# The second norm's inverse root moved from ScalarE and VectorE to ScalarE alone, and the prompt's top-8 rounds one place earlier

## The chip, the cores and the metric

The kernel runs on one core of a Trainium2 chip. The metric is the device time of one execution in microseconds (us), as the median of several runs. TensorE multiplies matrices, VectorE (DVE in the trace) and ScalarE (ACT) work on vectors, GpSimd (POOL) issues the indirect DMAs, SyncE (SP) the others. Each engine has its own instruction stream and waits for the others by semaphores.

## What is computed

Two layers of a mixed attention, convolution and MLP backbone with an expert-choice mixture of experts, for 256 prompt tokens and 1024 latent tokens of width 1024. The change concerns the second RMS norm of each layer and what routes the tokens:

```python
def rmsnorm(x, g):
    xf = x.astype(jnp.float32)
    y = xf * lax.rsqrt(jnp.mean(xf * xf, axis=-1, keepdims=True) + EPS)
    return (y * g.astype(jnp.float32)).astype(x.dtype)

def expert_choice_ffn(h, p):
    b, n, d = h.shape
    cap = (EC_FACTOR * n) // N_EXPERTS
    logits = jnp.einsum('bnd,de->bne', h, p['w_router']).astype(jnp.float32)
    aff = jax.nn.softmax(logits, axis=-1)
    gates, idx = lax.top_k(aff.transpose(0, 2, 1), cap)
    xs = jax.vmap(lambda hb, ib: hb[ib])(h, idx)
    ...

def layer_step(x, mod, rope, ctx_ckv, ctx_krope, p):
    ...
    x = x + g1 * mix
    h = rmsnorm(x, p['norm2_g']) * (1 + sc2) + sh2
    x = x + g2 * expert_choice_ffn(h, p)
    return x, ckv, kpe
```

With 16 experts and a factor of 2 each expert takes 32 prompt rows and 128 latent rows.

## The kernel before

The tokens stand in ten tiles of 128, two of the prompt and eight latent ones. In the stage that the change touches they are taken in the order latent first: s = 0 to 7 are latent tiles, s = 8 and 9 the prompt's. For each tile TensorE projects the mixer's output with w_out (L1177, 32 matmuls of 512 columns), VectorE multiplies by the gate and adds the residual (`add_residual`, L2030 and L2032, which gives XO), TensorE turns XO (L1189), and ScalarE takes the sum of squares of XO (`mean_square`, L1600) and copies the turned tile (`copy_sums`, L1562; for prompt tiles also L1565, for latent tiles VectorE does the second half, L2001). ScalarE then takes the square root of mean square plus eps (`root`, L1603) and signals `ss2_ready`. VectorE takes the reciprocal, rstd (`normalise_sums`, L2040), and writes the normalised tile XN (L2046); of the prompt's tiles ScalarE writes it (`normalise_prompt_sums`, L1610).

Beside that runs the router. TensorE multiplies the turned, not yet normalised tile by the weights in four parts (`route`, L1203), ScalarE copies the parts (`copy_parts`, L1574, behind `root` in its stream), TensorE adds them up (`add_parts`, L1218), and VectorE makes the logits by multiplying by rstd (`row_maxima`, L2007), takes the row maximum and its negative (L2010, L2011, nmax). ScalarE takes the exponents (`exponents_of`, L1580), VectorE their reciprocal sum and the affinities (`affinity`, L2016, L2019), TensorE turns the affinities (L1226) and ScalarE copies them (L1589) into `aff`: 32 partition rows for the latent tokens (two halves of 512 for each of 16 experts) and 16 more for the prompt's.

The selection is VectorE's. One round takes the eight largest of each partition row (MAX8, L2051), finds their positions (L2056) and overwrites them with -1 (L2057). The latent rows need 16 rounds, numbered 0 to 15; the prompt's rows need four, and these are done in the same instructions, on 48 partitions instead of 32. `PROMPT_ROUND` is the first of the four. They can start only when tile 9's affinities are there. The order on VectorE is written out by hand: rounds 0 and 1, rstd of tile 8, rounds 2 and 3, tile 8's logits, first half of tile 9's residual, tile 8's affinities, round 4, second half of tile 9's residual, rounds from 5 to `PROMPT_ROUND - 2`, rstd and logits of tile 9, MAX8 of round `PROMPT_ROUND - 1`, tile 9's affinities, the rest of that round, the four rounds with the prompt, the prompt's positions (L2099), one round, the prompt's index tables out of PSUM (idx_q, L2103 to L2105), the rest of the rounds, and the lists of the latent rows (L2107 to L2119).

Behind the tables GpSimd gathers the chosen prompt rows (L718, four indirect DMAs) from xnp_dram, TensorE turns them (`turn_prompt_rows`, L1239, in its stream behind the transposes of the lists, L1327 to L1330) and ScalarE modulates them (L1594). Behind the lists GpSimd gathers expert 0's latent rows (L723), TensorE turns them (L1342), ScalarE and VectorE modulate them (L1654, L2136), and the experts start (L1357). In layer 0 TensorE also computes part of layer 1's modulation in this tail (L1295, L1304).

ScalarE computes functions out of a loaded table; `ACT_TABLE_LOAD` instructions are put in by the build ahead of an ACTIVATE whose function is not in the loaded table.

Of the kernel before, what the change touches and what calls it, by code (L numbers as in the profile page):

```python
# [75 lines left out]
OUT_ORDER = list(range(PT, NT)) + list(range(PT))  # L76
ROUTED = [4, 5, 6, 7, 8, 9]
HALF = NS // 2
PROMPT_ROUND = 8
XQ_BANK = (4, 6, 2, 4)  # L80
PROMPT_LIST = slice(CAP_P + 8 * PROMPT_ROUND, 2 * CAP_P + 8 * PROMPT_ROUND)

# [32 lines left out]
def backbone(nc, x_prompt, x_sample, cache_ckv, cache_krope, c, c_ctx, w_ada, b_ada, norm1_g, norm2_g, w_in,  # L115
# [8 lines left out]
    with ExitStack() as ctx:  # L124
# [3 lines left out]
        def sem(name):  # L128
            return ctx.enter_context(nc.semaphore(name))
# [246 lines left out]
        h2_turned = sem("h2_turned")  # L376
        h2_ready = sem("h2_ready")
        log_summed = sem("log_summed")
        row_scalar_ready = sem("row_scalar_ready")
        lexp_ready = sem("lexp_ready")  # L380
        aff_ready = sem("aff_ready")
        aff_turned = sem("aff_turned")
# [1021 lines left out]
        def _(act):  # L1404
# [10 lines left out]
            for l in range(DEPTH):  # L1415
# [160 lines left out]
                def exponents_of(t):  # L1576
                    if not 0 <= t < NT:
                        return
                    act.wait_ge(row_scalar_ready, at(l, NT + PT, t + 1 + max(0, t + 1 - NT + PT)))
                    act.activation(logit[:, t % 2, :], logit[:, t % 2, :], ACT.Exp, bias=nmax[:, t % 2:t % 2 + 1],  # L1580
                                   accum_out=psum_row[:, t % 2:t % 2 + 1]).then_inc(lexp_ready, 1)

# [14 lines left out]

                def mean_square(s):
                    act.wait_ge(xo_ready, at(l, NT, s + 1))
                    own.done(act.activation(junk_d, XO[s % 2], ACT.Square, accum_out=ss_act[:, s:s + 1]))  # L1600

                def root(s):
                    act.activation(ss[:, s:s + 1], ss_act[:, s:s + 1], ACT.Sqrt, bias=eps[:, :], scale=1.0 / D)\  # L1603
                        .then_inc(ss2_ready, 1)

                def normalise_prompt_sums(s):

                    act.wait_ge(row_scalar_ready, at(l, NT + PT, s + 1 + s - NT + PT))
                    act.wait_ge(xn_stored[s % 2], at(l, 16 * NT // 2, 16 * (s // 2)))
                    act.activation(XN[s % 2], XO[s % 2], ACT.Copy, scale=rstd[:, s:s + 1]).then_inc(xn2_ready, 1)  # L1610

                for s in range(NT + 1):
                    copy_sums(s - 1)
                    if s:
                        root(s - 1)
                    copy_parts(s - 1)
                    exponents_of(s - 1)
                    copy_affinity(s - 1)
                    if s > NT - PT:
                        normalise_prompt_sums(s - 1)  # L1620
                    if s < NT:
                        mean_square(s)
# [76 lines left out]
        def _(dve):  # L1699
# [46 lines left out]
            for l in range(DEPTH):  # L1746
# [256 lines left out]
                def row_maxima(t):  # L2003
                    tile = OUT_ORDER[t]
                    i, g = t % 2, 0 if tile < PT else 1
                    dve.wait_ge(sel_summed, at(l, NT, t + 1))
                    dve.scalar_tensor_tensor(out=logit[:, i, :], in0=PS[:, 7, 0:E], scalar=rstd[:, t:t + 1],  # L2007
                                             in1=const_row[:, g, :], op0=ALU.mult, op1=ALU.add).then_inc(logit_ready, 1)
                    dve.wait_ge(logit_ready, at(l, NT, t + 1))
                    step(dve.tensor_reduce(pmax[:, i:i + 1], logit[:, i, :], AX, ALU.max))  # L2010
                    dve.tensor_scalar(nmax[:, i:i + 1], pmax[:, i:i + 1], -1.0, None, ALU.mult).then_inc(row_scalar_ready, 1)  # L2011

                def affinity(t):
                    tile, i = OUT_ORDER[t], t % 2
# [22 lines left out]

                def normalise_sums(s):
                    dve.wait_ge(ss2_ready, at(l, NT, s + 1))
                    step(dve.reciprocal(rstd[:, s:s + 1], ss[:, s:s + 1]))  # L2040
                    if s >= NT - PT:
                        dve.sem_inc(row_scalar_ready, 1)
                        return
                    if s >= 2:
                        dve.wait_ge(xn_stored[s % 2], at(l, 16 * NT // 2, 16 * (s // 2)))
# [194 lines left out]
```

## Time and profile before

| | us |
|---|---|
| median of 3 runs | 2514.78 (2513.65 to 2514.93) |
| the profiled execution's own time | 2514.64 |
| its span in the profile | 2512.9 |
| TensorE (PE) busy | 2402.1, 96% of the span |
| VectorE (DVE) busy | 771.1 |
| ScalarE (ACT) busy | 510.4 |

The chain of work that ended last is 93% TensorE and 3% VectorE. A row of the groups by line names line, engine, operation, what is written and read, the shapes and the count, then the busy time, the mean of one in ns, and the idle time of the engine before them. A row of the timeline is start, duration, engine and line; in brackets the idle time before it and what ended it. A row of the stretches gives for each engine the busy time and the count of instructions.

### The profile page before, as it was taken

The page shows a single profiled execution, that of the slowest core. Times are in us where ns is not written, and L with a number is a line of the kernel's source. Part 1 is how long each engine was busy: PE and PEld are TensorE (multiplying, and loading weights), DVE is VectorE, ACT ScalarE, POOL GpSimd, SP SyncE. Part 2 cuts the span into 40 slices and gives each one's busy share as a digit, 9 for nine tenths or more (in the row PEclk, how much of TensorE's full clock was granted, in tenths as well). Part 3 has the DMA queues.
Part 4 walks back from the last instruction along what each step waited for, and adds up shares of the span by engine and source line. Part 5 has one row for each costly group of instructions (what it writes and reads, how often), then busy time and mean ns, then how long its engine had stood idle before and what let it go on. Part 6 is the DMA issues. An engine that isn't in the chain of part 4 may idle for free.

```text
span 2512.9 us, 31572 instructions
## 1 busy us (share of the span) xinstructions
PE 2402.1 (96%) x13056; PEld 1587.0 (63%) x13056; DVE 771.1 (31%) x1553; ACT 510.4 (20%) x1038; POOL 277.1 (11%) x434
## 2 busy tenths in 40 slices
PE   6999999999998999999989999999999959999996
PEld 4545556666444788788845455666654448888785
DVE  2401334455237211111142022445543361111113
ACT  3310122222234201101142102212223331011103
POOL 3000011201000111211110000110000001211211
PEclk8999999999999999999999999999999979999998
DMA  9100224301426788888850002330012258888888
GB/s 327 34 17 5 84 74 133 88 10 51 176 101 234 264 276 273 273 277 271 271 171 17 21 0 84 110 110 11 9 65 106 87 193 271 277 274 271 277 282 302
DMA packets 165724, 388.07 MB, mean 154 GB/s; under 512 B 14544, under 2 KB 24984, under 8 KB 165632
## 3 DMA queue, kind: packets, MB, share of 16 engines
q1 hardware_dynamic: 142864, 332.48, 38.8%
q0 software_dynamic: 22768, 54.29, 9.0%
q8 instruction: 66, 1.08, 0.2%
q14 instruction: 26, 0.21, 0.1%
HBM read 339.09 MB, written 47.65 MB: 154 GB/s over the span
## 4 chain that ended last, share of the span: by engine, by line
PE 93%; DVE 3%; DMA 2%; ACT 1%; issue 1%; SPq 0%; DVEq 0%; POOLq 0%; ACTq 0%
PE PS L1357 11%; PE PS L1364 11%; PE PS L1177 11%; PE PS L1389 9%; PE PS L930 8%; PE PS L1023 7%; PE PS L1088 7%; PE PS L884 5%; PE PS L873 5%; PE PS L1070 4%; PE PS L1035 4%; PE PS L1383 2%; PE PS L984 1%; PE PS L1342 1%; PE PS L1048 1%; DMA r<-in_x_prompt_dram 1%
## 5 line engine op out<-in xcount | busy, mean ns | idle before, releaser
L1357 PEld LDWEIGHTS PS<-r,ring 128*128 128x128 f32 x2048 | 281.5, 190 | 16.8 <-issue 16.8
L1177 PE MATMUL PS<-ring,mix 128*128 128x512 f32 x640 | 288.4, 598 | 1.2 <-DVE mix L1928 1.2
L1357 PE MATMUL PS<-r,ring 128*128 128x160 f32 x2048 | 283.6, 299 | 2.0 <-ACT r L1654 2.0
L1364 PE MATMUL PS<-r,ring 128*128 128x160 f32 x2048 | 283.4, 299 | 0.0
L1364 PEld LDWEIGHTS PS<-r,ring 128*128 128x128 f32 x2048 | 279.9, 190 | 0.0
L1389 PE MATMUL PS<-ring,r 128*128 128x512 f32 x496 | 221.1, 599 | 0.0
L930 PE MATMUL PS<-r,ring 128*128 128x512 f32 (+1 forms) x576 | 208.4, 521 | 1.6 <-ACT r L1457 1.6
L1023 PE MATMUL PS<-lat,r 128*128 128x512 f32 (+1 forms) x416 | 203.6, 587 | 4.8 <-ACT r L1500 2.7
L1177 PEld LDWEIGHTS PS<-ring,mix 128*128 128x128 f32 x640 | 116.4, 190 | 129.7 <-issue 129.7
L1882 DVE COPY r<-PS 128x512 f32<-128x512 f32 x200 | 138.3, 692 | 188.3 <-PE PS L1070 188.3
L1088 PE MATMUL PS<-r 128*128 128x256 f32 x768 | 188.7, 381 | 0.0
L2148 DVE TENSOR_TENSOR r<-r,PS 128x320 f32<-128x320 f32 x64 | 31.2, 488 | 498.0 <-PE PS L1364 498.0
L1088 PEld LDWEIGHTS PS<-r 128*128 128x128 f32 x768 | 141.2, 190 | 51.1 <-issue 37.3
L930 PEld LDWEIGHTS PS<-r,ring 128*128 128x128 f32 x576 | 109.1, 190 | 100.6 <-issue 95.0
L1389 PEld LDWEIGHTS PS<-ring,r 128*128 128x128 f32 x496 | 91.7, 190 | 116.6 <-issue 116.6
L1514 ACT ACTIVATE r<-PS,nmax 128x1536 f32<-128x1536 f32 x64 | 98.7, 1542 | 318.3 <-DVE nmax L1875 313.3
L884 PE MATMUL PS<-ring,r 128*128 128x512 f32 x320 | 140.0, 592 | 0.0
L1070 PEld LDWEIGHTS PS<-ident,r 128*128 128x128 f32 x800 | 96.3, 141 | 66.9 <-issue 51.5
L1871 DVE TENSOR_REDUCE pmax<-PS 128x1 f32<-128x1536 f32 x64 | 112.2, 1753 | 75.3 <-PE PS L1035 75.0
L873 PE MATMUL PS<-ring,r 128*128 128x448 f32 x320 | 126.0, 547 | 0.5 <-DVE r L1759 0.5
L1070 PE MATMUL PS<-ident,r 128*128 128x128 f32 x800 | 121.3, 274 | 3.5 <-DVE r L1882 2.1
L1665 ACT ACTIVATE r<-PS 128x320 f32<-128x320 f32 x64 | 24.5, 434 | 479.7 <-PE PS L1357 479.7
(305 smaller groups left out, 2176.5 us busy)
## 6 DMA issues: line engine op xcount, KB each, us to landing
ring<-in_w_gate_dram SPq DMA_DIRECT2D x32, 2048.0 KB, 10.1
ring<-in_w_up_dram SPq DMA_DIRECT2D x32, 2048.0 KB, 10.6
ring<-in_w_down_dram SPq DMA_DIRECT2D x31, 2048.0 KB, 9.8
ring<-in_w_ada_dram SPq DMA_DIRECT2D x17, 2048.0 KB, 10.0
x_dram<-r SPq DMA_DIRECT2D x20, 512.0 KB, 2.9
r<-x_dram SPq DMA_DIRECT2D x20, 512.0 KB, 4.2
r<-in_x_sample_dram SPq DMA_DIRECT2D x16, 512.0 KB, 4.2
ring<-in_w_in_dram SPq DMA_DIRECT2D x4, 2048.0 KB, 12.4
```

Source lines behind the costliest of these rows:

```text
L873: ins = pe.matmul(psum(4 + t % 2, 448), hT[:, k, t * P:(t + 1) * P], W_IN[0][:, k, :], start=(k == 0), stop=(k == KD - 1))
L884: ins = pe.matmul(psum(t % 4, 512), hT[:, k, t * P:(t + 1) * P], W_IN[1][:, k, :], start=(k == 0), stop=(k == KD - 1))
L930: ins = pe.matmul(psum(base + j, tn), W_IN[u][:, k, c0:c0 + P], hT[:, k, t0:t0 + tn], start=(k == 0), stop=(k == KD - 1))
L1023: ins = pe.matmul(psum(3 * slot + c, w), QA[:, 2 * ITEMS[n][0] + slot, q], CKV[:, keys], start=(slot == 0), stop=(slot == 1))
L1070: ins = pe.transpose(PS[:, 6, j * P:(j + 1) * P], Pr[slot][:, (4 * r + j) * P:(4 * r + j + 1) * P], ident[:, :])
L1088: ins = pe.matmul(PS[:, 7, 0:256], CKVT[:, PT + k, :], PTr[:, :, k, :], start=(k == 0), stop=(k == 11))
L1177: ins = pe.matmul(psum(2 * (s % 2) + n, 512), mix[:, k, tile * P:(tile + 1) * P], W_OUT[n][:, k, :], start=(k == 0), stop=(k == KD - 1))
L1357: ins = pe.matmul(PS[:, b // 2, (b % 2) * 256:(b % 2) * 256 + SLOTS], W_G[:, k, b * P:(b + 1) * P], XST[par][:, k, :], start=(k == 0), sto ...
L1364: ins = pe.matmul(PS[:, 2 + b // 2, (b % 2) * 256:(b % 2) * 256 + SLOTS], W_U[:, k, b * P:(b + 1) * P], XST[par][:, k, :], start=(k == 0), ...
L1389: ins = pe.matmul(psum(4 + n, 512), HID[:, k, 0:CAP_S], w_down[:, k, n * 512:(n + 1) * 512], start=(k == 0), stop=(k == 3))
L1871: ins = dve.tensor_reduce(pmax[:, c:c + 1], psum_wide(3 * slot, KEYS_S), AX, ALU.max)
L1882: dve.tensor_copy(PTr[:, slot, 4 * r:4 * r + 4, :], psum(6, 512).rearrange("p (k q) -> p k q", q=P))\
```

## The change

The sum of squares is scaled inside the Square (by 1/sqrt(1024)), so that it is a mean. `root` becomes `inverse_root`: ScalarE takes the logarithm of mean plus eps, waits for itself, and takes exp(-0.5 x), which is rstd; only then does it signal `ss2_ready`. VectorE's reciprocal goes, and with it the second use of `row_scalar_ready`, which is renamed. `PROMPT_ROUND` becomes 7. Code of the changed kernel lies up to two lines further down than that of the kernel before.

```diff
-PROMPT_ROUND = 8
+PROMPT_ROUND = 7
...
                 def exponents_of(t):
                     if not 0 <= t < NT:
                         return
-                    act.wait_ge(row_scalar_ready, at(l, NT + PT, t + 1 + max(0, t + 1 - NT + PT)))
+                    act.wait_ge(lmax_ready, at(l, NT, t + 1))
...
                 def mean_square(s):
                     act.wait_ge(xo_ready, at(l, NT, s + 1))
-                    own.done(act.activation(junk_d, XO[s % 2], ACT.Square, accum_out=ss_act[:, s:s + 1]))
-
-                def root(s):
-                    act.activation(ss[:, s:s + 1], ss_act[:, s:s + 1], ACT.Sqrt, bias=eps[:, :], scale=1.0 / D)\
-                        .then_inc(ss2_ready, 1)
+                    own.done(act.activation(junk_d, XO[s % 2], ACT.Square, scale=float(D) ** -0.5,
+                                            accum_out=ss_act[:, s:s + 1]))
+
+                def inverse_root(s):
+
+                    own.done(act.activation(ss[:, s:s + 1], ss_act[:, s:s + 1], ACT.Ln, bias=eps[:, :], scale=1.0))
+                    act.activation(rstd[:, s:s + 1], ss[:, s:s + 1], ACT.Exp, scale=-0.5).then_inc(ss2_ready, 1)
 
                 def normalise_prompt_sums(s):
 
-                    act.wait_ge(row_scalar_ready, at(l, NT + PT, s + 1 + s - NT + PT))
+                    act.wait_ge(ss2_ready, at(l, NT, s + 1))
                     act.wait_ge(xn_stored[s % 2], at(l, 16 * NT // 2, 16 * (s // 2)))
...
                     copy_sums(s - 1)
                     if s:
-                        root(s - 1)
+                        inverse_root(s - 1)
                     copy_parts(s - 1)
...
-                    dve.tensor_scalar(nmax[:, i:i + 1], pmax[:, i:i + 1], -1.0, None, ALU.mult).then_inc(row_scalar_ready, 1)
+                    dve.tensor_scalar(nmax[:, i:i + 1], pmax[:, i:i + 1], -1.0, None, ALU.mult).then_inc(lmax_ready, 1)
...
                 def normalise_sums(s):
                     dve.wait_ge(ss2_ready, at(l, NT, s + 1))
-                    step(dve.reciprocal(rstd[:, s:s + 1], ss[:, s:s + 1]))
                     if s >= NT - PT:
-                        dve.sem_inc(row_scalar_ready, 1)
                         return
```

ScalarE, layer 0, tile 9 (the last one), in the kernel before: from its sum of squares to the normalised tile.

```order
L1600 ACTIVATE r,ss_act<-r 128x1024
L1562 ACTIVATE r<-PS 128x512
L1565 ACTIVATE r<-PS 128x512
L1603 ACT_TABLE_LOAD
L1603 ACTIVATE ss<-ss_act,eps 128x1
L1574 ACTIVATE lat<-PS 128x128
L1580 ACT_TABLE_LOAD
L1580 ACTIVATE logit,psum_row<-logit,nmax 128x16
L1589 ACTIVATE lat<-PS 16x128
L1610 ACTIVATE r<-r,rstd 128x1024
```

The same place in the changed kernel:

```order
L1600 ACTIVATE r,ss_act<-r 128x1024
L1562 ACTIVATE r<-PS 128x512
L1565 ACTIVATE r<-PS 128x512
L1605 ACT_TABLE_LOAD
L1605 ACTIVATE ss<-ss_act,eps 128x1
L1606 ACT_TABLE_LOAD
L1606 ACTIVATE rstd<-ss 128x1
L1574 ACTIVATE lat<-PS 128x128
L1580 ACTIVATE logit,psum_row<-logit,nmax 128x16
L1589 ACTIVATE lat<-PS 16x128
L1612 ACTIVATE r<-r,rstd 128x1024
```

The second table load stands ahead of the new exponent and of the parts' copy (L1574), no longer behind it; the number of loads is the same for every tile.

VectorE, layer 0, in the kernel before: from the end of tile 9's residual (L2032) over rounds 5 and 6 to tile 9's logits (L2007).

```order
L2032 TENSOR_TENSOR r<-r 128x512
L2051 MAX lat<-lat 32x8
L2056 MAX_INDEX top_i<-lat 32x8
L2057 MATCH_REPLACE lat<-lat 32x512
L2051 MAX lat<-lat 32x8
L2056 MAX_INDEX top_i<-lat 32x8
L2057 MATCH_REPLACE lat<-lat 32x512
L2040 RECIPROCAL rstd<-ss 128x1
L2007 SCALAR_TENSOR_TENSOR logit<-PS,rstd,const_row 128x16
L2010 TENSOR_REDUCE pmax<-logit 128x1
```

The same place in the changed kernel:

```order
L2034 TENSOR_TENSOR r<-r 128x512
L2051 MAX lat<-lat 32x8
L2056 MAX_INDEX top_i<-lat 32x8
L2057 MATCH_REPLACE lat<-lat 32x512
L2009 SCALAR_TENSOR_TENSOR logit<-PS,rstd,const_row 128x16
L2012 TENSOR_REDUCE pmax<-logit 128x1
```

One round instead of two stands between the residual and the logits, and the reciprocal is gone; the round comes back behind the prompt's tables, where four rounds of 32 rows stand instead of three.

## Rows read from the trace of the kernel before

**Rows 1.** Stretches of time: busy us and count of each engine.

```profile
777.00:827.00 50.00, 35.17 (x523) 25.73 (x522) 41.37 (x112) 23.67 (x70) 5.23 (x6) 0.86 0.58 213
1852.00:2009.00 157.00, 155.51 (x580) 75.19 (x582) 51.57 (x105) 48.77 (x86) 0.00 (x0) 1.00 0.25 90
2009.00:2059.00 50.00, 21.04 (x131) 13.77 (x124) 40.85 (x112) 18.27 (x41) 5.22 (x6) 0.66 0.56 210
```

**Rows 2.** Groups by line and shape, ScalarE, and VectorE's reciprocal, the whole program.

```profile
L1603 ACT ACT_TABLE_LOAD x20 | 25.7, 1283 | 0.4
...
L1580 ACT ACTIVATE logit<-logit,nmax 128x16 f32<-128x16 f32 x20 | 6.1, 307 | 50.9 <-DVE nmax L2011 50.8
...
L1412 ACT ACTIVATE stat<-eps 128x1 f32<-128x1 f32 x2 | 0.4, 202 | 0.0
...
L2040 DVE RECIPROCAL rstd<-ss 128x1 f32<-128x1 f32 x20 | 3.3, 163 | 23.1 <-ACT ss L1603 23.0
```

**Rows 3.** Timeline, layer 1, tile 6: VectorE, ScalarE and VectorE again.

```profile
1976.35 0.17 DVE L2040 RECIPROCAL rstd<-ss 128x1 f32<-128x1 f32 x1 [1.59 <-ACT ss L1603]
...
1978.11 0.28 ACT L1574 ACTIVATE lat<-PS 128x128 f32<-128x128 f32 x1 [1.79 <-PE PS L1203]
...
1981.84 0.23 DVE L2007 SCALAR_TENSOR_TENSOR logit<-PS,rstd,const_row 128x16 f32<-128x16 f32 x1 [4.53 <-PE PS L1218]
```

**Rows 4.** Timeline, layer 1, tile 8: root, reciprocal, rounds 2 and 3, logits.

```profile
2007.94 0.29 ACT L1603 ACTIVATE ss<-ss_act,eps 128x1 f32<-128x1 f32 x1
2008.34 0.17 DVE L2040 RECIPROCAL rstd<-ss 128x1 f32<-128x1 f32 x1 [0.34 <-ACT ss L1603]
2008.66 0.68 DVE L2051 MAX8 lat<-lat 32x8 f32<-32x512 f32 x1 [0.16 <-DVE rstd L2040]
...
2010.94 0.68 DVE L2051 MAX8 lat<-lat 32x8 f32<-32x512 f32 x1
...
2013.34 0.23 DVE L2007 SCALAR_TENSOR_TENSOR logit<-PS,rstd,const_row 128x16 f32<-128x16 f32 x1 [0.15 <-PE PS L1218]
```

**Rows 5.** Timeline, layer 1, tile 9: from the four parts to the logits.

```profile
2022.16 1.08 PE L1203 MATMUL PS<-r,lat 128*32 128x128 f32 x16 [1.23 <-ACT r L1565]
...
2023.42 0.29 ACT L1603 ACTIVATE ss<-ss_act,eps 128x1 f32<-128x1 f32 x1
2023.62 0.26 ACT L1574 ACTIVATE lat<-PS 128x128 f32<-128x128 f32 x1
2023.90 1.28 ACT L1580 ACT_TABLE_LOAD   x1
...
2023.93 0.61 PE L1218 MATMUL PS<-sel,lat 128*128 128x16 f32 x2 [0.69 <-ACT lat L1574]
2023.96 0.16 DVE L2040 RECIPROCAL rstd<-ss 128x1 f32<-128x1 f32 x1
2024.58 0.23 DVE L2007 SCALAR_TENSOR_TENSOR logit<-PS,rstd,const_row 128x16 f32<-128x16 f32 x1 [0.45 <-PE PS L1218]
```

**Rows 6.** Timeline, layer 0, tile 9: TensorE's four parts, their sum, and the logits.

```profile
790.32 0.64 PE L1203 MATMUL PS<-r,lat 128*32 128x128 f32 x16 [1.22 <-ACT r L1565]
...
792.09 0.40 PE L1218 MATMUL PS<-sel,lat 128*128 128x16 f32 x2 [1.13 <-ACT lat L1574]
...
792.74 0.23 DVE L2007 SCALAR_TENSOR_TENSOR logit<-PS,rstd,const_row 128x16 f32<-128x16 f32 x1 [0.16 <-DVE rstd L2040]
```

**Rows 7.** Chain of waits that ended last (start, us, what): layer 0, then layer 1.

```profile
817.76 6.12 DMA r<-xn_dram,idx_g
...
2049.99 5.71 ACT r L1594 x16
...
2058.40 0.47 issue
```

**Rows 8.** Timeline: ScalarE's 16 blocks in layer 0, VectorE's blocks in layer 1.

```profile
818.15 5.70 ACT L1594 ACTIVATE r<-PS,mod_all,scale_all 128x128 f32<-128x128 f32 x16 [7.74 <-PE PS L1239]
...
2057.22 1.36 DVE L2136 TENSOR_SCALAR r<-PS,scale_all,mod_all 128x128 f32<-128x128 f32 x4
```

More of the change, by code:

```diff
@@ L378, in backbone @@
         log_summed = sem("log_summed")
-        row_scalar_ready = sem("row_scalar_ready")
+        lmax_ready = sem("lmax_ready")
         lexp_ready = sem("lexp_ready")
```

## Prediction

> **What bounds the kernel now.** I read the stretches first. While the ten token tiles are projected, 1852 to 2009 us in layer 1, TensorE is busy 155.5 of 157.0 us: whatever the other engines do there is hidden as long as TensorE does not wait for it. In the 50 us that follow, from tile 8's routing to the first expert, TensorE is busy 35.2 us in layer 0 and 21.0 us in layer 1, and VectorE 41.4 and 40.9 us [rows 1]. So the change has one kind of place where it counts, twice in the program: the tail between the last projections and the first expert, where VectorE runs 16 top-8 rounds (three operations each) one behind the other. A round takes 2.28 us, from one MAX8 at 2008.66 to the next at 2010.94 [rows 4]. The timeline of the tail shows VectorE without a pause except 0.34 + 0.16 us around tile 8's reciprocal, 0.15 us before tile 8's logits and 0.45 us before tile 9's [rows 4, 5]. In the tail VectorE is the bound, and what makes it wait there, or moves rounds to where they no longer fill a wait, is paid in full.
>
> **What the change does on ScalarE.** Table loads: the kernel before has two for each tile (20 at L1603, 1.28 us each [rows 2], and as many for the logits' exponent at L1580), and the build of the changed kernel still has two: one ahead of the logarithm and now a second ahead of the exponent that gives rstd, while the one ahead of the logits' exponent goes. The count stays, the place moves. Before, the second load ran while ScalarE waited for VectorE's nmax anyway; now it stands between the sum of squares and rstd. A load starts 0.02 us behind the instruction before it (the parts' copy ends at 2023.88, the load starts at 2023.90) and is taken to hold up its ACTIVATE by 0.02 more [rows 5]. Logarithm with eps: as the square root it replaces, 0.29 [rows 5]. The exponent has no bias column: 0.20, as L1412's ACTIVATE without one; the upper bound is the logits' exponent with one, 0.31 [rows 2]. From the end of the old square root to the end of the new exponent: 0.02 + 1.28 + 0.02 + 0.20 = **1.52 us**.
>
> A rule of the skill speaks of both points. The rows show loads back to back with the instruction before them, 1.28 us each [rows 2, 5]. The Trainium skill, "ScalarE: Activation LUTs", section "What ACT_TABLE_LOAD costs", agrees on about 1283 ns but adds some 1380 ns of drain to every switch. By that price the four second loads that are exposed would cost 5.5 us more; the trace shows no such gap.
>
> **Tiles 0 to 7: nothing.** There ScalarE has 1.79 us between the square root and the copy of the parts (L1574), and the load and exponent take 1.52. VectorE's scaling of the tile into XN starts 1.3 us later, inside the 4.53 us in which VectorE waits for TensorE's L1218 [rows 3]. Cover: 0.27 us on ScalarE; if it were gone, L1574 would still have the 3 us until L1218. VectorE's reciprocal (0.17) was inside the same wait. The store of XN moves 1.3 us, with nobody waiting for it before the gathers.
>
> **Tile 8 (first prompt tile): the wait gets longer.** VectorE finishes two rounds at 2008.00 and waits 0.34 us, then does the reciprocal and a step to itself, and starts round 2 at 2008.66. Now rstd comes at 2007.94 + 0.29 + 1.52 = 2009.75, and VectorE sees it some 0.11 us later, as it does now (2008.23 to 2008.34): 2009.86 instead of 2008.66, **+1.20**, with the reciprocal's 0.32 already taken off [rows 4]. Behind it on VectorE are rounds 2 and 3, tile 8's logits, tile 9's residual and everything else. The logits had waited 0.15 us for TensorE [rows 4] (taken for both layers), which the delay uses up but for 0.01: **+1.04** from there on. The residual of tile 9 and so TensorE's and ScalarE's last pass move with it.
>
> **Tile 9: the chain to its logits.** Square, copies, table load, square root at 2023.42, parts' copy at 2023.62, L1218 at 2023.93, logits at 2024.58, with the last step a wait of 0.45 [rows 5]. The parts' copy now starts behind logarithm and exponent: from the start of the root 0.29 + 0.02 + 1.28 + 0.02 + 0.18 = 1.79 instead of 0.20, **+1.59**. In layer 1 the logits come at +1.04 + 1.59 = **+2.63**. In layer 0 L1218 ends at 792.49, so the logits could have started at 792.52, yet VectorE, late itself, starts them at 792.74: 2.63 counts from 792.52, which makes **+2.41** [rows 6]. Nothing fills the wait. VectorE had finished round 6 at 2023.94 [rows 5] and now stops one round earlier: round 5 ends at 2023.94 - 2.28 + 1.04 = 2022.7, the logits come at 2027.2, 4.5 us idle.
>
> **The prompt's rounds, 8 to 11 by count from one.** PROMPT_ROUND 7 for 8 takes one round from ahead of tile 9's logits and puts it behind the prompt's tables. The 16 rounds stay 16. Where VectorE waits for the logits anyway, a round in front is free and one behind costs its 2.28 us. So the prompt's tables (idx_q) come at +2.4 and +2.6, and the lists of all experts at **+4.69** (layer 0) and **+4.91** (layer 1).
>
> **What is next.** The first expert needs the lists: TensorE turns them, then the prompt rows, ScalarE modulates 16 blocks (5.7 us without a pause), TensorE turns expert 0's rows. These move as one. Two small things come back. In layer 0 TensorE was also waiting for the gather of xn rows, 817.76 + 6.12 = 823.88, with ScalarE done at 823.85 [rows 7, 8]; the gather now shares the DMA engines less with the up weights, whose start moves by 2.4 only, so its landing stops being the last: -0.13. In layer 1 VectorE's blocks of expert 0 (2057.22, 1.36 us) ended behind ScalarE's, which shows as 0.47 us of issue before the first matmul; they were late because the prompt rows' gathers were, and these now have 2.28 us more before the lists: -0.34 [rows 7, 8]. Layer 0: 4.69 - 0.13 = 4.56. Layer 1: 4.91 - 0.34 = 4.57. From there TensorE runs the experts without a break, so nothing is given back.
>
> **Sum.** 2514.64 (the profiled execution's own time, 0.14 under the median of 2514.78) + 9.13 = **2523.8 us**, +0.36%. Own range of this case: 0.11 more for each of four exponents up, tile 8's delay absorbed in both layers (-2.1) down, about 1.5 us of small shifts either way: 2520.5 to 2526.
>
> **Rivals.**
> (a) *Logarithm and exponent run from one table set, no load between them.* Not slower by what can be measured. For it: it is what would make the edit sensible. Against: the built list has the load. The price: tile 8 finds rstd ready, but its logits wait for TensorE as before; tile 9's parts' copy then waits for L1203 only, which ends at 2023.24 and 790.96, and starts 0.05 later instead of at 2023.62 and 791.78 (0.31 before L1218's start at 792.09) [rows 5, 6]. That puts the logits at -0.33 (layer 1) and, as the wait they had left is used up, -0.77 - 0.22 = -0.99 (layer 0), plus 2.28 each for the moved round, less 0.13: +3.1, **2517.7**. It decides from the point where rstd comes before VectorE has finished its rounds. The Trainium skill, same page, section "Table sets: the hidden batching unit", says this: one set holds both, so logarithm then exponent need one load.
> (b) *The prompt rows, not the lists, set the first expert.* Then only the tables' delay counts: 2.41 + 2.63 = 5.0, **2519.7**. For it: the gathers are the last of several things. Against: ScalarE's 16 blocks begin right behind the lists' transposes and never pause.
> (c) *A load between two dependent ACTIVATEs costs twice*, since ScalarE first has to empty: one more load's length, 1.28, in the four exposed places, +5.1, **2528.9**. For it: the rows have no load between two ACTIVATEs of which one reads the other's result. Against: the load of tile 9 starts 0.02 us behind the copy before it [rows 5]. The drain in the section cited above is this rule.
> (d) *Faster*: the reciprocals and the earlier prompt tables free VectorE and the gathers. Twenty reciprocals are 3.3 us, four of them in the tails, 0.7 us in all [rows 2]; it would need the one set as well and gathers that end last.
>
> **Chances.** Forecast 0.80, (a) 0.07, (b) 0.05, (c) 0.05, (d) 0.01, something else slower 0.02. A measurement of this kernel tells about 0.2% (5.0 us) from no change. Faster 0.02, same 0.10, slower 0.88. The range leaves out (a), (c) and part of the rest: 2519.3 to 2527.5.
>
> **What would show it.** In the profile of the changed kernel: two table loads of 1.28 us a tile, both ahead of the parts' copy; tile 8's third round starting 1.2 us later behind its second; VectorE idle 4 to 4.5 us before tile 9's logits, put down to TensorE's L1218; four rounds of 32 rows behind idx_q instead of three; the tables at +2.4 to +2.6 and the first expert at +4.6 in each layer; everything else in its place. Wrong if the load before rstd is missing or longer, if VectorE's idle time before tile 9's logits stays under 2 us, or if the first expert moves by much less than the lists.

## The result and the profile after

The changed kernel takes **2524.62 us** (median of 5 runs, 2523.54 to 2527.08), the kernel before on the same chip 2514.93 (5 runs, 2513.65 to 2515.55). The ratio is 1.0041, 95% interval 1.0030 to 1.0052: slower by 9.7 us, twice what a measurement of this kernel can tell. The forecast was 2523.8. The profiled execution took 2523.54, its span is 2521.8 against 2512.9.

The page gives the first impression that such a change leaves: almost none.

```profile
PE 2404.3 (95%) x13056; PEld 1591.6 (63%) x13056; DVE 767.9 (30%) x1533; ACT 513.9 (20%) x1058; POOL 276.3 (11%) x434
```

TensorE has 2.2 us more busy time than before, VectorE 3.2 less (the 20 reciprocals, 3.3), ScalarE 3.5 more. So the time is idle time. The groups by line of ScalarE show what was built: two loads for each of the 20 tiles, both now ahead of rstd, and a new exponent of 203 ns.

```profile
L1605 ACT ACT_TABLE_LOAD x20 | 25.7, 1283 | 0.3
L1606 ACT ACT_TABLE_LOAD x20 | 25.7, 1283 | 0.4
...
L1606 ACT ACTIVATE rstd<-ss 128x1 f32<-128x1 f32 x20 | 4.1, 203 | 0.2
```

**Tiles 0 to 7**, timeline of layer 1, tile 7. VectorE waits longer for rstd (it was 1.59 us at the same place of tile 6 [rows 3]) and shorter for TensorE's L1218, and ScalarE still waits 0.27 us for the four parts: the load is covered, with the 0.27 to spare that the prediction gave.

```profile
1996.74 0.75 DVE L2046 TENSOR_SCALAR r<-r,rstd 128x1024 f32<-128x1024 f32 x1 [3.11 <-ACT rstd L1606]
1996.98 0.28 ACT L1574 ACTIVATE lat<-PS 128x128 f32<-128x128 f32 x1 [0.27 <-PE PS L1203]
2000.71 0.23 DVE L2009 SCALAR_TENSOR_TENSOR logit<-PS,rstd,const_row 128x16 f32<-128x16 f32 x1 [3.22 <-PE PS L1218]
```

**Tile 8**, layer 1. Logarithm, load and exponent stand 0.02 us apart, and VectorE's third round waits 1.86 us, where it waited 0.34 + 0.16 with a reciprocal between [rows 4].

```profile
2011.10 0.29 ACT L1605 ACTIVATE ss<-ss_act,eps 128x1 f32<-128x1 f32 x1
2011.41 1.28 ACT L1606 ACT_TABLE_LOAD   x1
2012.70 0.20 ACT L1606 ACTIVATE rstd<-ss 128x1 f32<-128x1 f32 x1
...
2013.01 0.68 DVE L2051 MAX8 lat<-lat 32x8 f32<-32x512 f32 x1 [1.86 <-ACT rstd L1606]
```

**Tile 9**, layer 1: VectorE, one round short, is idle 4.69 us (4.25 in layer 0) before the logits, where it waited 0.45 [rows 5].

```profile
2027.80 0.29 ACT L1605 ACTIVATE ss<-ss_act,eps 128x1 f32<-128x1 f32 x1
2028.11 1.28 ACT L1606 ACT_TABLE_LOAD   x1
2029.40 0.20 ACT L1606 ACTIVATE rstd<-ss 128x1 f32<-128x1 f32 x1
2029.51 0.26 ACT L1574 ACTIVATE lat<-PS 128x128 f32<-128x128 f32 x1
...
2029.82 0.61 PE L1218 MATMUL PS<-sel,lat 128*128 128x16 f32 x2 [2.20 <-ACT lat L1574]
2030.57 0.23 DVE L2009 SCALAR_TENSOR_TENSOR logit<-PS,rstd,const_row 128x16 f32<-128x16 f32 x1 [4.69 <-PE PS L1218]
```

**From the lists to the first expert**, TensorE, layer 1, and then the same end in layer 0:

```profile
2055.09 0.31 PE L1327 MATMUL PS<-ident,lat 32*128 32x32 f32 x1 [11.09 <-DVE lat L2107]
...
2064.00 1.09 PE L1342 MATMUL PS<-ident,r 128*128 128x128 f32 x8 [2.36 <-ACT r L1594]
...
2066.86 9.83 PE L1357 MATMUL PS<-r,ring 128*128 128x160 f32 x64 [0.34 <-ACT r L1656]
```

```profile
829.27 1.67 PE L1342 MATMUL PS<-ident,r 128*128 128x128 f32 x8 [2.63 <-ACT r L1594]
830.73 1.92 PE L1239 MATMUL PS<-ident,lat 128*128 128x128 f32 x8
832.61 9.15 PE L1357 MATMUL PS<-r,ring 128*128 128x160 f32 x64
```

**How I compare the traces.** All times of a layer are counted from the start of tile 7's logits there, the last event that both kernels reach in the same way. In us:

| after tile 7's logits | before L0 / L1 | after L0 / L1 | difference L0 / L1 | predicted |
|---|---|---|---|---|
| third round | 11.09 / 11.11 | 12.31 / 12.30 | +1.22 / +1.19 | +1.20 |
| tile 8's logits | 15.78 / 15.79 | 16.86 / 16.86 | +1.08 / +1.07 | +1.04 |
| tile 9's logits | 26.74 / 27.03 | 29.43 / 29.86 | +2.69 / +2.83 | +2.41 / +2.63 |
| prompt's tables | 41.52 / 41.82 | 44.22 / 44.65 | +2.70 / +2.83 | +2.4 / +2.6 |
| lists (L1327) | 48.98 / 49.27 | 53.95 / 54.38 | +4.97 / +5.11 | +4.69 / +4.91 |
| first expert (L1357) | 60.76 / 61.31 | 66.20 / 66.15 | +5.44 / +4.84 | +4.56 / +4.57 |
| its second half (L1364) | 69.56 / 70.11 | 75.19 / 75.82 | +5.63 / +5.71 | as above |

The chain of waits is of no use for this trace: it covers 2% of the span. The span can be put together without it, because three of its stretches are rigid. From layer 0's L1364 to that layer's last down projection (L1389) it is 419.34 us before and 419.35 after, from the third projection of layer 1 (L873) to tile 7's logits there 705.92 and 705.93, from layer 1's L1364 to the end 445.24 and 445.27. What moves is the start of the tail in layer 0 (766.00 to 766.41), the two tails, and the layer change between L1389 and that third projection. Before: 766.00 + 69.56 + 419.34 + **36.73** + 705.92 + 70.11 + 445.24 = 2512.90. After: 766.41 + 75.19 + 419.35 + **33.83** + 705.93 + 75.82 + 445.27 = 2521.80. The tails cost 11.34, and 2.90 come back at the layer change.

That give-back is in these rows, GpSimd's wait for the last rows of layer 0 to land and TensorE's second projection of layer 1. Before:

```profile
1276.36 0.85 POOL L661 DMA_DIRECT2D mix<-in_cache_ckv_dram  x1 [10.59 <-DMA x_dram<-r,scol]
...
1282.65 7.95 PE L873 MATMUL PS<-ring,r 128*128 128x448 f32 x16 [0.28 <-DVE r L1759]
```

After:

```profile
1281.21 0.85 POOL L661 DMA_DIRECT2D mix<-in_cache_ckv_dram  x1 [9.39 <-DMA x_dram<-r,scol]
...
1287.48 6.25 PE L873 MATMUL PS<-ring,r 128*128 128x448 f32 x16 [0.27 <-DVE r L1761]
```

The rows landed 1.20 us sooner, and the same 16 matmuls took 1.70 less, because the granted clock was 1.00 instead of 0.78. The stretches of time that hold them (busy us and count of PE, PEld, DVE, ACT, POOL, then the granted clock, the share of the DMA engines, GB/s), before and after:

```profile
1282.60:1290.40 7.80, 7.75 (x16) 3.74 (x17) 3.23 (x10) 2.71 (x7) 0.00 (x0) 0.78 0.53 172
```

```profile
1287.40:1293.60 6.20, 6.12 (x17) 3.13 (x18) 3.23 (x10) 2.75 (x8) 0.00 (x0) 1.00 0.67 217
```

Both times of landing are counted from the start of L1389 (21.46 and 20.26 us). Whether that belongs to the change is taken up behind the experiments.

### The profile page after: what moved, and what is told of

It is laid out like the page before. It is cut to its first block and busy times, and to the rows that moved or that the text cites. A ratio compares the mean times of both kernels' runs of the same rounds, so it can differ in the third digit from the quotient of the medians.

```text
span 2521.8 us, 31568 instructions
## 1 busy us (share of the span) xinstructions
PE 2404.3 (95%) x13056; PEld 1591.6 (63%) x13056; DVE 767.9 (30%) x1533; ACT 513.9 (20%) x1058; POOL 276.3 (11%) x434
## 3 DMA queue, kind: packets, MB, share of 16 engines
q8 instruction: 66, 1.08, 0.2%
## 5 line engine op out<-in xcount | busy, mean ns | idle before, releaser
L1357 PEld LDWEIGHTS PS<-r,ring 128*128 128x128 f32 x2048 | 282.6, 191 | 15.4 <-issue 15.4
L1357 PE MATMUL PS<-r,ring 128*128 128x160 f32 x2048 | 284.7, 300 | 0.3 <-ACT r L1656 0.3
L1364 PE MATMUL PS<-r,ring 128*128 128x160 f32 x2048 | 283.4, 299 | 0.0
L1364 PEld LDWEIGHTS PS<-r,ring 128*128 128x128 f32 x2048 | 279.9, 190 | 0.0
L1389 PE MATMUL PS<-ring,r 128*128 128x512 f32 x496 | 221.1, 599 | 0.0
L1389 PEld LDWEIGHTS PS<-ring,r 128*128 128x128 f32 x496 | 91.8, 190 | 116.4 <-issue 116.4
L873 PE MATMUL PS<-ring,r 128*128 128x448 f32 x320 | 125.0, 544 | 0.5 <-DVE r L1761 0.5
```

The costliest lines, as they stand in the source:

```text
L873: ins = pe.matmul(psum(4 + t % 2, 448), hT[:, k, t * P:(t + 1) * P], W_IN[0][:, k, :], start=(k == 0), stop=(k == KD - 1))
L1357: ins = pe.matmul(PS[:, b // 2, (b % 2) * 256:(b % 2) * 256 + SLOTS], W_G[:, k, b * P:(b + 1) * P], XST[par][:, k, :], start=(k == 0), sto ...
L1364: ins = pe.matmul(PS[:, 2 + b // 2, (b % 2) * 256:(b % 2) * 256 + SLOTS], W_U[:, k, b * P:(b + 1) * P], XST[par][:, k, :], start=(k == 0), ...
L1389: ins = pe.matmul(psum(4 + n, 512), HID[:, k, 0:CAP_S], w_down[:, k, n * 512:(n + 1) * 512], start=(k == 0), stop=(k == 3))
```

## The experiments

The theory is the prediction's: a table load that stands between the sum of squares and rstd delays VectorE twice in each tail, and a round moved behind the prompt's tables fills no wait and costs its length. Its rivals are (a) one table set, (b) gathers that set the expert, (c) a load that costs twice. All medians are set against the kernel before on the same chip: 2515.53 (31 runs) for before_pr7, after_pr8 and the two oneset kernels, 2515.42 (15 runs) for double_load and warm_less, 2515.57 (20 runs) for the other four. The column of the tails is the sum of both tails, up to L1364, over that of before, from one trace each. It lies above the medians' difference in every row, by 0.5 us (before_pr7) to 5.4 (double_load). All rows use the one trace of before, and in that one the stretch from expert 0's rows on ran at the full clock in both layers, while its layer change is the longest of the twelve: its split is not a typical one. Compare the tails with each other rather than with the medians.

| kernel | runs | median | over before | ratio, 95% | tails | layer change |
|---|---|---|---|---|---|---|
| before | 5 | 2514.93 | 0 | | 0 (139.67) | 36.73 |
| after | 5 | 2524.62 | +9.69 | 1.0041 [1.0030, 1.0052] | +11.34 | 33.83 |
| before_pr7 | 10 | 2520.48 | +4.95 | 1.0018 [1.0008, 1.0027] | +5.48 | 33.72 |
| after_pr8 | 10 | 2520.95 | +5.42 | 1.0020 [1.0010, 1.0030] | +8.89 | 35.27 |
| oneset_pr7 | 10 | 2518.74 | +3.21 | 1.0010 [1.0001, 1.0020] | +6.18 | 35.89 |
| oneset_pr8 | 10 | 2514.51 | -1.02 | 0.9994 [0.9985, 1.0004] | +1.19 | 34.58 |
| late_wait | 5 | 2523.24 | +7.67 | 1.0032 [1.0018, 1.0046] | +8.48 | 35.48 |
| after_pr9 | 10 | 2520.64 | +5.07 | 1.0024 [1.0014, 1.0034] | +8.18 | 34.22 |
| warm_after | 4 | 2530.56 | +14.99 | 1.0062 [1.0046, 1.0079] | +20.25 | 33.93 |
| warm_oneset_pr8 | 10 | 2518.93 | +3.36 | 1.0012 [1.0002, 1.0022] | +8.12 | 35.90 |
| double_load | 4 | 2530.12 | +14.70 | 1.0057 [1.0042, 1.0072] | +20.09 | 33.54 |
| warm_less | 11 | 2513.78 | -1.64 | 0.9995 [0.9986, 1.0004] | +1.89 | 36.16 |

### The two parts apart: before_pr7 and after_pr8

The kernel before with the changed rounds alone, and the changed kernel with the old rounds.

```diff
-PROMPT_ROUND = 8
+PROMPT_ROUND = 7
```

> The kernel before with PROMPT_ROUND 7 alone, the square root and the reciprocal kept. Theory: tile 9's logits wait for TensorE's sum as before, 2.28 us of VectorE stand idle instead of a round, the lists come 2.28 us later in layer 1 and 2.06 in layer 0: about 2519.2 us. Rival (the prompt's tables set the first expert, and these come no later): 2514.9.

```diff
-PROMPT_ROUND = 7
+PROMPT_ROUND = 8
```

> The changed kernel with PROMPT_ROUND 8 instead of 7, the table loads where the change puts them. Theory: VectorE waits 4.5 us before tile 9's logits anyway, so the round in front is free and the one behind is saved: the logits come when they came with 7, the lists 2.28 us earlier in each layer, about 2520 us. Rival (the round's place does not matter): 2524.6.

Measured: +4.95 for the rounds alone, +5.42 for the norm alone, 10.4 together, and +9.69 with both. The two parts add up as far as their intervals (some 2.5 us to either side) can show, and each is about half. In before_pr7, layer 1, VectorE has finished its rounds early. It is idle for 1.89 us ahead of the reciprocal, which waits for the root, and for 0.60 ahead of the logits, and gets them hardly sooner, since TensorE's sum of the parts ends about when it did (the logits start 27.03 after tile 7's before, 26.76 here):

```profile
2025.07 0.23 DVE L2007 SCALAR_TENSOR_TENSOR logit<-PS,rstd,const_row 128x16 f32<-128x16 f32 x1 [0.60 <-PE PS L1218]
```

The lists then come 2.28 and 2.00 us later than before (51.26 and 51.27 for 48.98 and 49.27): about the whole round, where 2.06 and 2.28 were expected. In layer 1 the eight transposes of tile 9 (L1189), which stand ahead of the parts, took 1.11 us for 1.38. In after_pr8 the same place shows that the round back in front fills the wait but for what the loads had added; its tile 9 logits stand at 29.43 and 30.30 (29.43 and 29.86 in the changed kernel), its lists at 52.28 and 52.54, 1.67 and 1.84 earlier than there. Both miss the 2.28 for reasons other than the round's length. In layer 0 VectorE has the lists (L2107) 2.28 sooner, 51.34 for 53.62, but TensorE turns them 0.6 late, behind a piece of layer 1's modulation in its stream (L1304; more on it under after_pr9). In layer 1 the transposes of tile 9 took 1.97 us for 1.53, and the logits came 0.44 later for it.

```profile
2030.08 0.23 DVE L2009 SCALAR_TENSOR_TENSOR logit<-PS,rstd,const_row 128x16 f32<-128x16 f32 x1 [2.85 <-PE PS L1218]
```

### Rival (a) made true: oneset_pr7 and oneset_pr8

The set that holds both logarithm and exponent is loaded by name ahead of the attention's exponents, which it serves too, so that the build sees no need for another up to the end of the stage.

```diff
+                act.preload_act_table_set("natural_log_exp_and_others")
                 for n in range(NI):
```

> The changed kernel, with the set that holds logarithm and exponent together loaded once per layer ahead of the attention's exponents: no table load in the stage at all, PROMPT_ROUND still 7. The loads between sum of squares and rstd are the cause of the longer waits (theory): tile 8 finds rstd ready, tile 9's logits come earlier than before by about 0.3 us in layer 1 and 1.0 in layer 0, and what remains is the moved round, 2.28 us in each layer: about 2518 us, lists of all experts at +1.9 and +1.3 against before. Rival: the logarithm, the exponent and the step between them cost as such: then it stays near 2524.6, VectorE's idle time before tile 9's logits above 4 us.

> As the run with one set, with PROMPT_ROUND back at 8. Theory (loads and the moved round are all there is): 2.28 us less in each layer than with 7, so 0.3 to 1.0 us a layer below the kernel before: about 2513.6 us. Rival (the place of the round costs nothing, VectorE would idle there anyway): same time as with 7.

In the groups by line of oneset_pr7 the 40 loads of the stage are gone, and with them the two at L1511 that the attention's exponents had. Two take their place, one for each layer, at L1540:

```profile
L1668 ACT ACT_TABLE_LOAD x15 | 19.2, 1283 | 0.3
L1412 ACT ACT_TABLE_LOAD x2 | 2.6, 1283 | 0.0
L1540 ACT ACT_TABLE_LOAD x2 | 2.6, 1283 | 0.0
```

Measured: +3.21 with the changed rounds, where rival (a) had +3.1, and -1.02 with the old ones, no measurable difference from the kernel before. The lists of oneset_pr7 came at +1.44 in layer 0 and +2.38 in layer 1, where 1.3 and 1.9 were expected. So the reciprocals' removal and the one-set norm are worth nothing that can be measured, and the loads of the stage are worth 9.69 - 3.21 = 6.5 us with the changed rounds and 5.42 + 1.02 = 6.4 with the old. That is both loads of each tile, the logarithm's too, and so more than the one that the change moved; that one alone is what after_pr8 and double_load measure. The same step of the timeline without the load, oneset_pr8, layer 1, tile 9:

```profile
2021.18 0.29 ACT L1606 ACTIVATE ss<-ss_act,eps 128x1 f32<-128x1 f32 x1
2021.50 0.20 ACT L1607 ACTIVATE rstd<-ss 128x1 f32<-128x1 f32 x1
2022.49 0.28 ACT L1575 ACTIVATE lat<-PS 128x128 f32<-128x128 f32 x1 [0.79 <-PE PS L1203]
...
2023.57 0.23 DVE L2010 SCALAR_TENSOR_TENSOR logit<-PS,rstd,const_row 128x16 f32<-128x16 f32 x1 [1.04 <-PE PS L1218]
```

rstd is ready at 2021.70, before TensorE has the parts, and the parts' copy now waits for TensorE. So in layer 1 the earliest point at which tile 9's logits can come is TensorE's, and it lies later than in the kernel before (27.42 after tile 7's logits for 27.03), because the transposes of tile 9 took 1.97 us here and 1.38 there. In layer 0 the logits start when VectorE has finished round 6, without a wait (26.42 for 26.74): there the old rounds leave nothing more to win.

### Rival (c): double_load

A third load in the chain, made by an ACTIVATE of another function between logarithm and exponent, whose result nobody reads.

```diff
                     own.done(act.activation(ss[:, s:s + 1], ss_act[:, s:s + 1], ACT.Ln, bias=eps[:, :], scale=1.0))
+                    act.activation(stat[:, 0:1], eps[:, :], ACT.Sqrt)
                     act.activation(rstd[:, s:s + 1], ss[:, s:s + 1], ACT.Exp, scale=-0.5).then_inc(ss2_ready, 1)
```

> The changed kernel with one more table load between sum of squares and rstd: a square root of a constant, read by nobody, between logarithm and exponent (its table, then the exponent's again). Theory (what stands between the sum of squares and rstd is paid in full at the prompt's two tiles): 1.28 + 0.02 + 0.20 = 1.5 us more at tile 8 and 1.5 more at tile 9, in both layers, so 6 us more than the changed kernel, about 2530.5; tile 9's logits at +3.0 against the changed kernel. Rival (a load only costs where it displaces the one for the logits' exponent): 2524.6 to 2526.

Measured: 2530.12, +14.70 over before on its chip, which is 5.0 more than the changed kernel's +9.69. Timeline, layer 1, tile 9:

```profile
2034.76 0.20 ACT L1606 ACTIVATE stat<-eps 128x1 f32<-128x1 f32 x1
2034.97 1.28 ACT L1607 ACT_TABLE_LOAD   x1
2036.27 0.20 ACT L1607 ACTIVATE rstd<-ss 128x1 f32<-128x1 f32 x1
```

An added load and its ACTIVATE take 1.51 us (2034.76 to 2036.27): 0.20 + 0.01 + 1.28 + 0.02. Tile 8's logits move by just that, +18.36 for +16.86. VectorE's third round waits 3.36 instead of 1.86. There is no drain beside the load, neither before it nor after it. The Trainium skill, "ScalarE: Activation LUTs", section "What ACT_TABLE_LOAD costs", states about 1283 ns for the load, which the rows show, and some 1380 ns of drain for each switch, which they don't: the loads stand between their neighbours here with gaps of 0.01 to 0.02 us. With four more exposed places at 1.51, 6.0 us were due; the median shows 5.0, the two tails of this one trace 8.75 (20.09 - 11.34), of which the lists carry 3.00 and 3.72 (3.02 were due; 0.44 of the excess in layer 1 is the transposes of tile 9, 1.97 us for 1.53) and the rest lies behind them.

### Tile 8's wait taken out: late_wait

VectorE waits for tile 8's rstd behind rounds 2 and 3, not ahead of them.

```diff
                 rounds(0, 2, 2 * E)
-                normalise_sums(NT - 2)
                 rounds(2, 4, 2 * E)
+                normalise_sums(NT - 2)
                 row_maxima(NT - 2)
```

> The changed kernel, with VectorE's wait for tile 8's rstd put behind rounds 2 and 3, right ahead of tile 8's logits, which are the first to read it there. Theory: tile 8's wait (1.86 us in the changed kernel, 0.34 + 0.16 before) is a cost of its own of about 1.05 us in each layer: the logits of tile 8 come when they came in the kernel before, tile 9's 1.05 earlier than in the changed kernel, about 2522.5 us. Rival (tile 9's chain on ScalarE sets everything behind it, whatever VectorE does at tile 8): 2524.6.

Tile 8's logits are back at 15.81 in both layers, tile 9's come at 28.16 and 28.72 (29.43 and 29.86 with the wait), the lists at 53.02 and 53.22, 0.93 and 1.16 earlier than in the changed kernel. That is the prediction's +1.04 for tile 8, carried to the lists in both layers. The medians give 2.0 of it back (7.67 for 9.69), with intervals that overlap.

### One round more in front: after_pr9

```diff
-PROMPT_ROUND = 7
+PROMPT_ROUND = 9
```

> The changed kernel with PROMPT_ROUND 9: rounds 5, 6 and 7 ahead of tile 9's logits, which fills the wait of 4.3 to 4.7 us there almost whole. The lists of all experts come at about +0.6 us against the kernel before, in both layers. If the lists set the first expert, 2516 us. If the prompt rows do, whose index tables are now only 5 us ahead of the lists instead of 7.4 (in layer 1 of the kernel before the second group of rows was turned 11 us after its table): about 2 to 3 us more in each layer, 2520 to 2522 us.

The wait before tile 9's logits is almost filled (0.57 in layer 1), and the lists of layer 1 come at 50.25, only 0.98 later than before. Yet the first expert comes at 65.72, no sooner than in after_pr8 (65.18). What takes the lists' place stands in TensorE's timeline, layer 1:

```profile
2052.78 1.97 PE L1239 MATMUL PS<-ident,r 128*128 128x128 f32 x8 [1.92 <-DMA r<-xnp_dram,idx_q]
2055.48 1.97 PE L1239 MATMUL PS<-ident,r 128*128 128x128 f32 x8 [0.74 <-DMA r<-xnp_dram,idx_q]
2058.20 1.97 PE L1239 MATMUL PS<-ident,lat 128*128 128x128 f32 x8 [0.75 <-DMA lat<-xnp_dram,idx_q]
2061.24 1.94 PE L1342 MATMUL PS<-ident,r 128*128 128x128 f32 x8 [1.07 <-DMA r<-xn_dram,idx_g]
```

The gathers end last, which is rival (b) in the main: TensorE waits for the prompt rows' gathers three times. ScalarE's 16 blocks, which follow these transposes, end at 2060.48, and the gather of expert 0's own rows, issued at 2052.26, lands 0.6 later still, at 2061.11. None of this is true of the changed kernel, whose transposes follow the lists without a wait. In layer 0 something else was late, the piece of layer 1's modulation that stands ahead of the lists in TensorE's stream. VectorE had the lists at 49.37 there, 1.97 sooner than in after_pr8, and TensorE turned them at 52.77, 0.49 later:

```profile
817.95 0.48 PE L1304 MATMUL PS<-ident,r 128*128 128x128 f32 x1 [4.47 <-ACT r L1631]
819.28 0.28 PE L1327 MATMUL PS<-ident,lat 32*128 32x32 f32 x1 [0.86 <-issue]
```

So from 7 to 8 the round is worth 1.67 and 1.84 in the lists and 4.3 us in the median for both layers (9.69 and 5.42), and from 8 to 9 nothing that can be measured (5.42 and 5.07).

### Is the rest TensorE's clock? warm_after, warm_oneset_pr8, warm_less

The part between lists and expert runs at a changing clock: the eight transposes of a row block take 1.04 to 1.10 us at the full clock (granted clock 1.00) and 1.91 to 1.97 at half (0.50), and something between where the clock changes on the way. In these three kernels TensorE multiplies constants, into a bank that nobody reads, while it would wait for the tables and the lists.

```diff
+                def keep_busy(n):
+
+                    for _ in range(n):
+                        pe.matmul(psum(3, 512), ones[:, :], cos_tok[:, :, :].rearrange("p t d -> p (t d)"), start=True,
+                                  stop=True)
```

> The changed kernel, with extra matmuls that nobody reads (ones times the cosine table into a free PSUM bank) in TensorE's idle time of the tail: 8 before the lists in layer 0, 12 before the prompt's tables and 14 before the lists in layer 1. Theory: part of the change's cost is TensorE starting at the lower of its two clock levels after the longer idle time; transposes of the prompt rows then take 0.9 us less per eight, expert 0's first 64 matmuls 8.7 instead of 9.2 and 9.8, in all about 3 us less than the changed kernel, 2521.5. Rival: the clock costs nothing that matters, and the extra matmuls only get in the way: 2524.6 or more.

> One table set, PROMPT_ROUND 8, and extra matmuls in TensorE's idle time of the tail (5 before the lists in layer 0; 12 before the tables and 10 before the lists in layer 1). Theory: on top of the 1 us that the one set gives against the kernel before, TensorE restarts at the higher clock level: 2 to 3 us less, about 2512. Rival: 2514.5, as without them.

> One table set, PROMPT_ROUND 8, and fewer extra matmuls in TensorE's idle time: none in layer 0, 8 before the prompt's tables and 6 before the lists in layer 1. Theory: the clock is up in layer 1 when the lists come and nothing is held up, so the way from the lists to expert 0 is 11.5 to 11.8 us instead of 12.6; layer 0 as with the one set alone: about 1 us less than the one set with 8, 2513.5. Rival (the earlier run with extra matmuls was late for another reason than their length): above 2516 again.

In the first two the extra work was too long. A matmul of constants took some 0.9 us (14 of them are 28 records and 12.28 us in the row below), so the work ran into the tables' and the lists' time. In warm_after, layer 1:

```profile
2051.66 12.28 PE L1309 MATMUL PS<-cos_tok,ones 128*128 128x512 f32 x28
2063.87 0.24 PE L1336 MATMUL PS<-ident,lat 32*128 32x32 f32 x1
```

The lists stand at 57.66 instead of 54.38 there, and at 60.89 instead of 53.95 in layer 0. One stretch is of use, warm_oneset_pr8, layer 1, where the lists were only 0.73 late (50.39 for 49.66):

```profile
2055.01 1.07 PE L1239 MATMUL PS<-ident,r 128*128 128x128 f32 x8
2057.01 1.09 PE L1239 MATMUL PS<-ident,r 128*128 128x128 f32 x8 [0.93 <-DMA r<-xnp_dram,idx_q]
2059.67 1.97 PE L1239 MATMUL PS<-ident,lat 128*128 128x128 f32 x8 [1.56 <-DMA lat<-xnp_dram,idx_q]
```

The first two blocks of transposes run at full clock, TensorE then waits for the gathers, and the third block is at half again. From lists to expert it takes 11.82 instead of 12.64, 0.8 us less, with two of the five blocks at full clock; what a full clock all the way would give was not measured. In warm_less the matmuls ended 3.74 us before the lists; its transposes took 1.95 again, and its median, -1.64, can't be told from oneset_pr8's -1.02. That it would help to keep TensorE busy is not shown.

## Why the prediction was right, and where it was not

**The cover in tiles 0 to 7**: right, with the 0.27 us to spare that it named.

**The load's price, 1.52 us**: right. From the end of the logarithm to the end of the exponent it is 2011.39 to 2012.90, 1.51. The load that moved is 1.28, two gaps are 0.02. Rival (c) is out by double_load.

**Tile 8**: predicted +1.20 and +1.04, measured +1.22 / +1.19 and +1.08 / +1.07 (the prediction's own terms, 1.20 less the 0.14 of the wait that is used up, give 1.06); late_wait takes it out again.

**Tile 9**: the logits came at +2.69 and +2.83, not +2.41 and +2.63. The step of +1.59 is not what was short: from the start of root or logarithm to the parts' copy it is 1.71 us for 0.20 in both layers, +1.51. What was short is TensorE's part, taken to cost the same as before. In layer 0 it was 0.75 us from the start of the sum of the parts to the logits, where 0.43 had been enough (792.09 to 792.52 [rows 6]); the sum itself took 0.61 instead of 0.40. In layer 1 the parts began 25.83 us after tile 7's logits, where they began 24.61 after them before: 1.07 later by the delay and 0.15 more by the transposes of tile 9, which ran at a granted clock of 0.67 instead of 0.74. Before and after:

```profile
2019.55 1.38 PE L1189 MATMUL PS<-ident,r 128*128 128x128 f32 x8 [2.68 <-DVE r L2032]
```

```profile
2023.78 1.53 PE L1189 MATMUL PS<-ident,r 128*128 128x128 f32 x8 [3.30 <-DVE r L2034]
```

The last 0.10 lies between the sum and the logits (0.75 us for 0.65). The same eight transposes took 1.11 us in before_pr7 and 1.97 in oneset_pr8, behind the same 2.7 us without work, so part of a microsecond in layer 1's logits goes with the clock of the single run.

**The moved round**: right, 2.28 in the lists (+4.97 - 2.69 and +5.11 - 2.83). before_pr7 shows it alone, 2.28 and 2.00 in the lists and 4.95 in the median, where 2.06 and 2.28 in the lists and about 4.3 in the time were expected.

**From the lists on** the prediction gave back 0.13 and 0.34. In layer 1 it was 0.27, and for the reason named: the gathers are no longer late, and VectorE's blocks of expert 0 start together with ScalarE's (both at 2065.13), where they started 0.34 behind them (2057.22 and 2056.88). In layer 0 the gather of xn rows did stop being the last [rows 7], and the way from the lists to expert 0's transposes is 0.13 shorter (8.91 for 9.04), but the whole stretch became 0.47 longer, 12.25 for 11.78. The eight transposes of expert 0's rows, 1.07 us before, took 1.67, and the eight behind them 1.92 instead of 1.04; the granted clock of that stretch was 0.56, for 1.00 before:

```profile
829.20:832.60 3.40, 3.33 (x16) 2.97 (x16) 1.55 (x5) 1.52 (x5) 0.00 (x0) 0.56 0.10 10
```

**"From there TensorE runs the experts without a break, so nothing is given back"** is the step that failed, twice and in opposite directions. The first 64 matmuls of expert 0 took 9.15 and 9.83 us, 8.96 both times before: another 0.19 and 0.87 lost to a clock that was not yet full (granted clock 0.98 and 0.91 over these matmuls, 1.00 both times before). And 2.90 came back at the layer change. The sum 9.13 stands beside a span that grew by 8.9, but by other terms: 0.41 ahead of the first tail, 11.34 in the two tails (9.13 predicted), -2.90 at the layer change, 0.03 at the end.

Is the give-back an effect of the change? Over the twelve traces the layer change takes 33.54 to 36.73 us: before_pr7 has 33.72 and before 36.73, after_pr8 35.27 and after 33.83. Two things differ in it. The clock on the second projection (7.95 us in before and after_pr8, 7.92 in oneset_pr7, 6.25 in after and before_pr7) goes with neither the norm nor the rounds; the 1.70 us are luck of the one trace, as far as can be seen. The landing of the last rows is less clear. In the three traces in which layer 0 ends earliest (L1389 before 1256 us: before, oneset_pr8, warm_less) it comes 21.0 to 21.5 us behind L1389, and in eight of the nine others 20.0 to 20.7 (the ninth, warm_oneset_pr8, has 21.1). So about 1 us of the give-back may well belong to any kernel that comes to this point later, and no run here decides it. Either way the agreement in the profiled span (9.13 for 8.9) is in part luck: 2.2 too little in the tails against 2.9 that nobody had forecast. The medians rest on more runs: +9.69, and the parts alone +4.95 and +5.42. What decides the clock's state in a given run stays open.

**The rivals.** (a) did not happen because the build chose otherwise. The edit itself is what would have made it true: with the joint set loaded by name, the loads go and the time falls by 6.5 us. The Trainium skill, same page, section "Table sets: the hidden batching unit", says that logarithm then exponent need one load; that holds in the runs where the set is named, and not for this kernel, whose trace has a load ahead of each of the two. (b) is shown not to hold at 7; at 9 the gathers set the expert, in layer 1. (d) had its best chance in oneset_pr8, which has the one set and the old rounds, and is no faster that can be measured.

## What to carry to other kernels

Before a function is swapped for a chain of two on ScalarE, read in the built list where the table loads will stand, and ask whether one of them moves from a place where the engine waits to one where others wait for it: here the number of loads and the busy time hardly changed, and 5.4 us were lost. If two functions share a set, name the set; that alone was worth 6.5 us against the changed kernel, though against the kernel before it won nothing that could be measured. And a piece of VectorE's work in front of a wait is free up to the wait's length, while behind it it costs its length, so such a number is set anew whenever the wait changes, and only until another transfer ends last.

## What the runs showed of the hardware

- A table load costs 1.28 us and no more, also between two ACTIVATEs of which one reads the other's result: the rows of tiles 8 and 9 show gaps of 0.01 to 0.02 us on both sides, and in double_load one more load with its ACTIVATE moved VectorE's third round by 1.50 us.
- An ACTIVATE on 128x1 takes 0.29 us with a bias column and 0.20 without.
- The first work of TensorE behind some 10 us of waiting has no fixed price. The same eight transposes took from 1.04 us at the full granted clock (2.4 GHz) to 1.97 at half (1.2 GHz), expert 0's first 64 matmuls 8.95 to 10.00, and this differed between traces of nearly equal kernels. By this spread a small saving behind such a wait can't be forecast to better than about 1 us. Shorter waits show it too: behind 2.7 to 3.3 us without work the transposes of tile 9 took 1.11 to 1.97.
- Up to tile 8's logits the tail repeats within 0.02 us from trace to trace (16.85 or 16.86 in the four kernels with the second load and nothing else there); the layer change varies by 3.2 us over the twelve. A difference between two profiled spans has to be split at such points before it is explained.
